# Dealing small DMA loads over the samples of a gather loop: a hybrid decoder step on one Trainium2 core

## The reference, cut to what matters

```
# GLA over the prompt, chunk by chunk (here chunks of 128 tokens, 8 of them)
bcum  = cumsum(log_a)                      # per channel
o     = (q k^T * exp(pairwise decays)) v + (q * exp(bcum)) S
S_new = exp(b_end) * S + (k * exp(b_end - bcum))^T v

# NSA for the 8 samples, over their paged cache (2048 rows each)
nsa_past = cache_nsa_kv[l][page_table]     # slots: raw key, raw value, selection key, selection value
hid      = compression MLP over slots 0 and 1
scores   = q . slot 2                      # kept for the selection branch
v_blk    = slot 3                          # kept for the selection branch

# mLSTM step of the samples, in a later stage, needs these small operands
state_mlstm_n (8,4,64), state_mlstm_m (8,4), the input and forget gates of the samples, ml_gate_b
```

## Time and profile before

| | us |
|---|---|
| median of 3 runs | 1873.37 |
| the profiled execution's own time | 1873.04 |
| its span in the trace | 1871.0 |
| PE busy in the whole span | 1743.5 (93%) |
| turns 3, 4, 5 of the stage, each | 23.60 |
| from SP's `zq` load of turn 1 to that of turn 3 (two turns) | 61.63 |

### The profile page before, as it was taken

One profiled execution on the slowest core, in us unless ns is written; L12 is line 12 of the kernel. 1 busy time (PEld: TensorE's weight loads), 2 busy tenths in 40 slices (PEclk: granted clock), 3 DMA queues, 4 the chain that ended last, 5 costly groups with the idle time before them and its releaser, 6 DMA issues. The chain is left out here.

```text
span 1871.0 us, 32344 instructions
## 1 busy us (share of the span) xinstructions
PE 1743.5 (93%) x12895; PEld 1620.8 (87%) x12895; DVE 1052.0 (56%) x1876; ACT 632.0 (34%) x1141; POOL 175.2 (9%) x205
## 2 busy tenths in 40 slices
PE   6999999979999978998865899999999999999998
PEld 6999999968888766786732899999999999999998
DVE  6372683258777755665566666444444444444445
ACT  6523331047555544443342344111112111111111
POOL 1000000022222242223111100000000000000000
PEclk7999999969999989999676999999999999999999
DMA  7741264250000165665566562111111111111102
GB/s 187 115 106 34 64 174 147 91 158 24 14 2 1 46 217 180 230 233 185 119 124 224 155 190 69 46 45 45 45 45 45 45 45 45 45 45 45 45 23 91
DMA packets 180898, 177.18 MB, mean 95 GB/s; under 512 B 51564, under 2 KB 163268, under 8 KB 177140
## 3 DMA queue, kind: packets, MB, share of 16 engines
q1 hardware_dynamic: 173924, 132.92, 25.2%
q0 software_dynamic: 2304, 33.56, 4.7%
q10 hardware_dynamic: 4560, 9.18, 1.8%
HBM read 139.60 MB, written 40.23 MB: 96 GB/s over the span
## 5 line engine op out<-in xcount | busy, mean ns | idle before, releaser
L59 PE MATMUL pm<-hH,wuH 128*128 128x344 f32 x768 | 246.3, 321 | 0.0
L61 PE MATMUL pm<-hH,wuL 128*128 128x344 f32 x768 | 245.0, 319 | 0.0
L60 PE MATMUL pm<-hL,wuH 128*128 128x344 f32 x768 | 245.0, 319 | 0.0
L59 PE MATMUL pm<-hidH,weights 128*128 128x344 f32 x720 | 230.7, 320 | 0.0
L60 PE MATMUL pm<-hidL,weights 128*128 128x344 f32 x720 | 230.2, 320 | 0.0
L61 PE MATMUL pm<-hidH,weights 128*128 128x344 f32 x720 | 230.0, 319 | 0.0
L59 PE MATMUL pz<-hH,winH 128*128 128x344 f32 x600 | 200.1, 334 | 1.6 <-DVE hL L845 1.6
L60 PE MATMUL pz<-hL,winH 128*128 128x344 f32 x600 | 194.1, 323 | 0.0
L61 PE MATMUL pz<-hH,winL 128*128 128x344 f32 x600 | 194.0, 323 | 0.0
L3302 DVE SCALAR_TENSOR_TENSOR act<-pm,onat 128x344 f32<-128x344 f32 x96 | 49.3, 515 | 239.7 <-PE pm L61 239.3
L3313 DVE TENSOR_TENSOR onat<-pm,onat 128x344 f32<-128x344 f32 x256 | 128.9, 513 | 68.9 <-PE pm L61 68.9
(11 more groups left out here) (610 smaller groups left out, 3501.1 us busy)
## 6 DMA issues: line engine op xcount, KB each, us to landing
uact<-in_w_up_dram SPq DMA_DIRECT2D x15, 1024.0 KB, 6.9
hs<-in_w_down_dram SPq DMA_DIRECT2D x15, 1024.0 KB
raw<-in_w_in_dram SPq DMA_DIRECT2D x24, 512.0 KB, 3.8
hold<-vS_scratch SPq DMA_DIRECT2D x8, 1024.0 KB, 14.4
wo<-in_w_out_dram SPq DMA_DIRECT2D x12, 512.0 KB
act<-in_w_out_dram SPq DMA_DIRECT2D x12, 512.0 KB, 5.2
zT_scratch<-zb ACTq DMA_DIRECT2D x8, 516.0 KB, 2.6
hold<-in_x_prompt_dram SPq DMA_DIRECT2D x8, 512.0 KB, 3.8
```

The costliest lines, as they stand in the source:

```text
L59: nc.tensor.matmul(out, wH, mH, start=start and k == 0, stop=False)
L60: nc.tensor.matmul(out, wH, mL, start=False, stop=False)
L61: last = nc.tensor.matmul(out, wL, mH, start=False, stop=stop and k == n - 1)
```

## The change

SP's list in this stage is put in another order, and `load_small_steps` takes a part number. Nothing is computed otherwise, and no other engine's list changes.

```diff
-                    for half in range(2):
-                        sp.wait_ge(gathered[half], 16 * (s + 1))
-                        sp.dma_start(io["vS"][s, :, half * 8:half * 8 + 8, :]...,
-                                     kv[half][:, :, 3, :, :]).then_inc(v_stored[half], 16)
-                    for half in range(2):
-                        sp.wait_ge(sc_kept, 2 * s + half + 1)
-                        for u in range(4):
-                            sp.dma_start(sS[s * 8:s * 8 + 8, half, :, u, :], ...).then_inc(sc_stored[half], 16)
-                    if s == 1:
-                        load_small_steps(sp, io, at, small_in)
+                    keep_values(s, 0)
+                    if s:
+                        store_scores(s - 1, 1)
+                    keep_values(s, 1)
+                    store_scores(s, 0)
+                    if 1 <= s <= 5:
+                        load_small_steps(sp, io, at, small_in, s - 1)
+                store_scores(NS - 1, 1)
...
-def load_small_steps(sp, io, at, loads):
+def load_small_steps(sp, io, at, loads, part):
-    sp.dma_start(at["qk"]...)
-    for h in range(4):
+    if part == 0:
+        sp.dma_start(at["qk"]...)
+    for h in ((part,) if part < 4 else ()):
         # n0, m0, gi, gf of head h, as before
-    for h2 in range(2):
+    for h2 in (range(2) if part == 4 else ()):
         # gb, as before
```

More of the change, by code:

```diff
@@ L1670, in load_w1, with keep_values, store_scores @@
                                      io["w1S"].rearrange("p (j r w e) -> p j r w e", j=2, r=16, w=2)[:, j, at, :, :]).then_inc(w_in[half], 16)
+                def keep_values(s, half):
+                    sp.wait_ge(gathered[half], 16 * (s + 1))
+                    sp.dma_start(io["vS"][s, :, half * 8:half * 8 + 8, :].rearrange("p r (h d) -> p r h d", h=2),
+                                 kv[half][:, :, 3, :, :]).then_inc(v_stored[half], 16)
+                def store_scores(s, half):
+                    sp.wait_ge(sc_kept, 2 * s + half + 1)
+                    for u in range(4):
+                        sp.dma_start(sS[s * 8:s * 8 + 8, half, :, u, :], sst[32 * u:32 * u + 8, half, :].rearrange("h (f p) -> h f p", f=2)
+                                     ).then_inc(sc_stored[half], 16)
                 load_z(0)
@@ L1680, in _ @@
                         load_z(s + 1)
-                    for half in range(2):
-                        sp.wait_ge(gathered[half], 16 * (s + 1))
-                        sp.dma_start(io["vS"][s, :, half * 8:half * 8 + 8, :].rearrange("p r (h d) -> p r h d", h=2),
-                                     kv[half][:, :, 3, :, :]).then_inc(v_stored[half], 16)
-                    for half in range(2):
-                        sp.wait_ge(sc_kept, 2 * s + half + 1)
-                        for u in range(4):
-                            sp.dma_start(sS[s * 8:s * 8 + 8, half, :, u, :], sst[32 * u:32 * u + 8, half, :].rearrange("h (f p) -> h f p", f=2)
-                                         ).then_inc(sc_stored[half], 16)
-                    if s == 1:
-                        load_small_steps(sp, io, at, small_in)
+                    keep_values(s, 0)
[6 more added lines that the diff above has]
+                store_scores(NS - 1, 1)
                 sp.wait_ge(small_in, 16 * SMALL_STEP_LOADS)
@@ L2043, in place_small_steps @@
             "gf": sb("gfd", [P, HP, NS]), "gb": sb("gbd", [P, 2, HP])}
-def load_small_steps(sp, io, at, loads):
+def load_small_steps(sp, io, at, loads, part):
     zT = io["zT"]
-    sp.dma_start(at["qk"][:, :, :], zT[GQ:GQ + 4 * P, T:TT].rearrange("(j p) s -> p j s", p=P)).then_inc(loads, 16)
-    for h in range(4):
+    if part == 0:
+        sp.dma_start(at["qk"][:, :, :], zT[GQ:GQ + 4 * P, T:TT].rearrange("(j p) s -> p j s", p=P)).then_inc(loads, 16)
+    for h in ((part,) if part < 4 else ()):
         rws, hp = slice((h % 2) * 64, (h % 2) * 64 + 64), h // 2
```

## The result

The change makes the kernel **faster by 0.75%**: the ratio of its time to that of the kernel before is 0.9925, 95% interval 0.9908 to 0.9941; medians of 20 runs each 1861.41 and 1876.55 us. The forecast was 1877 and no change. The range held the time, because it reached down to a rival's case; the mechanism that the forecast rested on did not hold: the case called "hidden" came true, which it had put at 1858.6 to 1862.

A forecast was written before the change was run, and what follows sets the result against it. The prediction took the stage's undisturbed turns as bound by PE, with 14.43 us lost once to stalls and clock. 1873.04 - 14.4 (small loads moved) + 0 (interleaving) + 18.6 (gathers held) = 1877.2, forecast 1877 us, range 1858 to 1885.

The forecast's parts named there:

- hidden: Rival for the small loads beside gathers: engines alternate finely, `m0` costs under 2.1 us, no stall; 1858.6 to 1862 us, chance 0.28.
- SP blocked: Turn 2's value store waited behind 19 small loads, delaying a gather: 8.28 us stall, forecast to go.
- a gather held: A second-half gather beside the small loads took 14.3 us to land instead of 8.1: 2.05 us stall, forecast to go.
- Part 2: Values and scores interleaved in SP's list: no transfer added, later stores still in time, cost 0.
- cover: Time between storing the former sample's second-half scores and ScalarE's next copy of that half: some 6 us.
- Part 3: Small loads now beside first-half gathers, turns 1 to 5: 4.65 us a turn, four turns, +18.6 us; bounds 0 and 26.
- the one meeting in the trace: Before the change, a gather issued at 714.56 moved no packet until 719.5 while `m0` ran; 6.2 us late.
- Slack 2.1: First-half gather lands 13.5 us into the turn, PE wants it at 15.6: 2.1 us to spare.
- hold near 5: Delay of a first-half gather by one head's `m0`: 512 packets at 100 a us, 5.1 us.
- low stretch of the clock: PE at its lower clock after each stall, 1.65 us lost once a stall.
- `gb` at 0: Turn 5's two `gb` loads, 512 packets beside the first-half gather: between 0 and 4.65 us, taken as 0.
- the first rival: The rival also called hidden: small packets pass in the gather's gaps, PE never stalls; 1858.6 us, chance 0.28.

The follow-up runs named there:

- `m0` twice: The changed kernel with each `m0` load issued a second time, into a tile nothing reads: turns 1 to 5 132.15 us, median 1871.21 us, ratio 0.9983.

## Why the prediction was wrong

**Where the time was lost: right.** Two stalls and the clock behind them, 14.43 us; the change has given back 14.41. Both causes were named rightly too, SP blocked and a gather held, and the first was certain as said.

**Part 2, cost 0: right.** Its cover was not idle talk, though. The run with all scores behind the small loads shows that the former sample's scores are waited for, at 34.6 us in all; that the change stores them ahead of the small loads is what keeps this at nothing.

**Part 3: the step that failed** is the sentence "That `m0` now starts some 1.5 us after the gather's first bytes instead of just before does not help: each engine takes the batch between two of its nine gather packets." It does help, wholly. I had taken from the one meeting in the trace that an engine works off its 32 packets of `m0` in one piece, whichever came first, and so put the gather's delay at 5.1 us, the stall at 3.0 and the part at 18.6. Measured: the first-half gathers landed in 8.3 to 10.1 us instead of some 13, no stall, 0. A gather that flows gives way to one small packet for each of its own (105 to 104); these were `qk`'s or `n0`'s, so that `m0` mostly came up when the gather was through. That order is not what saves it, though: where `m0` itself or `gb` met a flowing gather, it passed one for one as well (50 to 50, 90 to 91) and PE did not wait.

The row that I read for it shows less than that. In the earlier trace rows 186 small packets went beside 40 of the gather, which fits engines that were through with `m0` beside others that were not, and so settles nothing. The same trace has the one for one just behind it, from 722.5 to 724.5 us, which no row of mine showed:

```profile
q0 software_dynamic: 53, 0.87, 101.2%
q1 hardware_dynamic: 46, 0.00, 1.3%
```

Order decides, by little time: `m0` issued 0.5 us or more after the gather (0.46 in `m0` twice, 1.2 to 1.7 in the change) held nothing, issued from 0.2 us after it to 1.1 us before it cost 3.0 to 6.9 us a turn.

**The sizes in part 3 were right**, for another kernel. Slack 2.1, hold near 5 and a low stretch of the clock gave 4.65 us a turn; with the small loads four stores earlier it measured 5.4, of which 3.7 are the stall and 1.7 the rest (1.65 forecast for the clock). `gb` at 0 was right for the change by luck: it was put there because the slack covers two short pieces, but it runs at about the same rate as `m0` (110 packets a us), and turn 5 pays 6.5 us in that other kernel.

**The rule of the Trainium skill** ("DMA: Bandwidth & Descriptors", Queues, rings and completion order), turns from queue to queue packet by packet, stood beside the first rival, and the time that came is that rival's: 1858.6 forecast, 1873.04 x 0.9925 = 1859.0 measured. Its round-robin agrees with the 105 to 104 packets after; its typical 9 to 17 descriptors a turn is not what that stretch shows, which is one. A whole batch that goes first when it has the head start (330 small packets and none of the gather in 3.3 us) its upper limit of 64 would allow, but it names no such rule of precedence; there the measurement decides.

What stays open: what in an engine makes the head start count, whether descriptors fetched ahead or something else. The packets' order shows that it is so, not how. Nor is it explained why reading the same words again is slow, or what the stray differences of some us between profiles outside the turns are.

## What to carry to other kernels

Small DMAs beside a large transfer were cheap here if they were issued half a us or more after it and dear if they were ahead of its first bytes; so place them by the large transfer's start, and look at which packets move in that stretch. Count what a load reads, not only its bytes: one that reads the same few words once for each partition ran at about 100 packets a us here, distinct words at 360 and more. When two edits look as if each should help, measure them apart: here 4.8 and 1.8 us alone, 14.4 together.

## What the runs showed of the hardware

Reading the same words again is slow across all 16 engines together: 89 to 116 packets a us for `m0`, 110 for `gb`, packets of 4 bytes each; `m0` filled from as many distinct words went at 360. No run shows apart how `gi` and `gf`, one run of 32 bytes read again, fare. A score store of 8 KB is issued by SP in 0.3 us (the median before), but in some 0.5 behind `zq` and two value stores: four of them take 2.14 us in turn 2. They are what keeps `m0` behind the gather: with them it is issued 7.0 us into turn 2, without them 4.3, and the gather at 5.2 in both.
